# Dilated attention on one core: which engine copies the result rows out of PSUM

## What is computed

```
for window, dilation in ((128, 1), (512, 4), (2048, 16)):
    # positions regrouped by residue mod dilation; a query sees the 128 keys before it and itself
    o_i, lse_i = dilated_window_attn(q, k, v, window, dilation)     # 12 heads of 64
    # inside: s = q k / 8, masked; m = max(s); p = exp(s - m); den = sum(p); lse = m + log(den); o = (p / den) v
mix_w = softmax(stack(lses), axis=0)
o = sum(mix_w[..., None] * stack(outs), axis=0)
attn_out = o * silu(g_attn)
```

## Time and profile before

| | |
|---|---|
| median of 3 runs | 2197.28 us (2194.53 to 2199.95) |
| the profiled execution, time | 2200.2 us |
| the profiled execution, span | 2198.3 us |
| mean granted clock of TensorE | 0.97 of full speed |
| PE busy | 2008.3 us (91%) |
| DVE busy | 1551.7 us (71%) |
| ACT busy | 982.3 us (45%) |
| POOL busy | 997.2 us (45%) |

### The profile page before, as it was taken

One profiled execution on the slowest core, in us unless ns is written; L12 is line 12 of the kernel. 1 busy time (PEld: TensorE's weight loads), 2 busy tenths in 40 slices (PEclk: granted clock), 3 DMA queues, 4 the chain that ended last, 5 costly groups with the idle time before them and its releaser, 6 DMA issues.

```text
span 2198.3 us, 44066 instructions
## 1 busy us (share of the span) xinstructions
PE 2008.3 (91%) x16552; PEld 1487.1 (68%) x16552; DVE 1551.7 (71%) x3563; ACT 982.3 (45%) x2123; POOL 997.2 (45%) x1064
## 2 busy tenths in 40 slices
PE   5999999997788999689999999999998988786998
PEld 3545867896787888579864443447877777665886
DVE  7714948856898456687968889564499999894422
ACT  4323334321787001233443444333299999782211
POOL 4312324364331899631444333343124888974222
PEclk9999999999899999899999999999999999998999
DMA  5451331246661334332232232114367878565442
GB/s 180 138 125 58 102 94 37 66 139 197 159 140 42 124 139 151 122 125 69 70 107 78 75 93 72 56 50 112 90 143 174 203 195 207 162 191 166 163 167 85
DMA packets 275859, 267.40 MB, mean 122 GB/s; under 512 B 38224, under 2 KB 227536, under 8 KB 275392
## 3 DMA queue, kind: packets, MB, share of 16 engines
q1 hardware_dynamic: 266992, 252.19, 40.3%
q10 hardware_dynamic: 6976, 6.90, 1.2%
q0 software_dynamic: 1680, 5.51, 0.7%
HBM read 171.22 MB, written 93.31 MB: 120 GB/s over the span
## 4 chain that ended last, share of the span: by engine, by line
PE 37%; DVE 19%; POOL 10%; issue 5%; DMA 2%; ACT 2%; SPq 0%; DVEq 0%; ACTq 0%; POOLq 0%
PE bank L445 18%; PE bank L3072 7%; PE bank L173 7%; DVE s2m L2921 5%; DVE p2l L2927 4%; POOL xr L1995 2%; POOL xr L1993 2%; POOL xr L2008 2%; PE bank L1637 1%; POOL xr L2010 1%; PE bank L1654 1%; PE bank L1628 1%; DMA cm<-scr_part 1%; DVE ptl L1710 1%; DVE w2s L379 1%
## 5 line engine op out<-in xcount | busy, mean ns | idle before, releaser
L173 PE MATMUL bank<-w1h,xh 128*128 128x256 f16 x768 | 211.7, 276 | 3.0 <-DVE s1st L1169 3.0
L173 PE MATMUL bank<-w1h,xl 128*128 128x256 f16 x768 | 211.7, 276 | 0.0
L173 PE MATMUL bank<-w1l,xh 128*128 128x256 f16 x768 | 211.6, 276 | 0.0
L2866 PE MATMUL bank<-ident,p2r 128*128 128x128 f32 x900 | 163.9, 294 | 50.2 <-DVE p2l L2927 43.3
L2866 PEld LDWEIGHTS bank<-ident,p2r 128*128 128x128 f32 x900 | 95.9, 143 | 107.5 <-DVE p2l L2927 105.0
L2927 DVE SCALAR_TENSOR_TENSOR p2l<-bank,p2h 128x512 f16<-128x512 f32 (+1 forms) x288 | 165.0, 573 | 2.4 <-ACT p2h L2893 2.3
L1179 DVE SCALAR_TENSOR_TENSOR bank<-ain,cw,bank 128x512 f32<-128x512 f32 x208 | 157.0, 755 | 8.0 <-ACT bank L1124 1.7
L2921 DVE CUSTOM_DVE_ANT_0 s2m<-bank,both,finv 128x256 f32<-128x256 f32 (+1 forms) x384 | 161.1, 460 | 0.0
L173 PE MATMUL bank<-w2h,xh 128*128 128x256 f16 x512 | 140.5, 274 | 14.8 <-DVE xl L851 13.7
L2900 ACT ACTIVATE p2r<-s2m,ob 128x128 f32<-128x128 f32 (+1 forms) x384 | 147.5, 436 | 13.6 <-DVE ob L2921 13.3
L2893 ACT ACTIVATE p2h<-bank 128x512 f16<-128x512 f32 (+1 forms) x288 | 144.3, 501 | 15.1 <-PE bank L2866 11.5
(11 more groups left out here) (450 smaller groups left out, 6383.6 us busy)
## 6 DMA issues: line engine op xcount, KB each, us to landing
scr_part<-ob SPq DMA_DIRECT2D x48, 264.0 KB, 3.3
cm<-scr_part SPq DMA_DIRECT2D x48, 264.0 KB, 4.5
v<-scr_v SPq DMA_DIRECT2D x192, 65.0 KB, 2.4
ax<-in_x SPq DMA_DIRECT2D x16, 512.0 KB, 6.0
xr<-in_x SPq DMA_DIRECT2D x16, 512.0 KB, 4.4
bx<-scr_x SPq DMA_DIRECT2D x16, 512.0 KB, 8.0
x2r<-scr_x SPq DMA_DIRECT2D x16, 512.0 KB, 4.3
out<-yo SPq DMA_DIRECT2D x16, 512.0 KB, 2.9
```

The source lines that it names most:

```text
L173: ins = nc.tensor.matmul(dst, x, y, start=k == 0 and m == 0, stop=k == n - 1 and m == 2)
L2866: ins = nc.tensor.transpose(bank[:, w * hh + 128 * c:w * hh + 128 * c + 128], p[:, hh, 128 * c:128 * c + 128], ident[:])
```

## The change

ACT now makes the row copies of all units with dilation 1 and 4. With dilation 16 the two engines go on taking turns.

```
             elif item[0] == "gather":
                 x = units[item[1]]
                 if x["g"] % 2 == 0:
-                    on_act = x["g"] % 4 == 2
+                    on_act = x["d"] < 16 or x["g"] % 4 == 2
                     n_row[not on_act] += 1
                     o_bank = obk.take(a_row.at(n_row[0]) if on_act else d_row.at(n_row[1]))
```

## The result

The changed kernel takes 2190.85 us, the median of 14 runs (2187.01 to 2197.22), against 2198.51 us for the kernel before, also of 14 (2194.53 to 2203.91). The ratio is 0.9963, with a 95% interval of 0.9953 to 0.9974: 7.7 us less, where 11.0 were forecast. It is faster by a little more than the 0.3% that a measurement of this kernel can tell. The profiled execution has a span of 2189.8 us, against 2198.3.

A forecast was written before the change was run, and what follows sets the result against it. VectorE was taken to bound the stage of dilated attention. By pair of heads the gains were 2.3 + 2.0 + 5.4 + 1.3 = 11.0 us, subtracted from the median of 2197.28: 2186.3 us, range 2181.0 to 2193.5.

The forecast's parts named there:

- ScalarE sets the pace: Rival: ScalarE bounds every group at its upper ends, no reserve used; 6.0 us won, 2191.3 us; chance 0.21.
- The price on VectorE: Each row copy on VectorE puts off its successor by 0.33 us; 48 copies give an upper bound of 16.0 us.
- The price on ScalarE: On ScalarE a copy costs 0.26 us; four units take 5.64 to 5.74 (dilation 1), 5.22 to 5.32 (dilation 4).
- 0.77 us to spare: Reserve between ScalarE's p2h ending and VectorE's p2l taking it up, which ScalarE's lag must first use up: 0.77 us.
- I take 0.4: First pair of heads, without mixes: ScalarE's lag less the reserve costs 0 to 0.5 us, taken as 0.4.
- Dilation 16 gives ScalarE time to catch up: In dilation 16 the split is unchanged, so ScalarE recovers its lag and only the first pair of heads pays.
- Second: 2.0: Second pair of heads: GpSimd still waits for VectorE; six copies count, the last two are lost, 2.0 us won.
- Third to fifth: 1.8 each: Third to fifth pairs of heads: three copies win 1.0 us, then GpSimd's waits allow 0.79: 1.8 each, 5.4 together.
- E and B of dilation 16: Mix steps on VectorE, reciprocal and min: VectorE waits 0.3 to 0.7 us more for GpSimd there from the second pair.
- the 0.79 that GpSimd was to leave between the two B: Between the mins of dilations 4 and 16, GpSimd's waits for VectorE, 0.24 + 0.55 us, limit the gain to 0.79.
- I take the middle, 1.3: Sixth pair of heads: 0 won if GpSimd sets the way until 1969 us, otherwise 2.67; the middle, 1.3, taken.
- nothing changes: Rival: a copy costs ScalarE its whole 370 ns; 2.6 us won at most, 2194.7 us; chance 0.06.

The follow-up runs named there:

- light runs: Two of the three weight products of each mix left out on GpSimd: in the kernel before 2190.39 us, in the changed kernel 2182.30 us.
- after_again: The changed kernel run once more, unaltered, as a base for later runs: 2191.28 us, 0.9972 of the kernel before.
- d1_only: Against the kernel before, only the copies of dilation 1 go to ScalarE (24 instead of 48), dilation 4 stays split: 2191.19 us, 0.9967.
- d4_only: Against the kernel before, only the copies of dilation 4 go to ScalarE: 2195.66 us, 0.9981.
- lead_11: The changed kernel with GpSimd's query copies issued 11 steps ahead instead of 12: 2194.02 us, 0.9979 of the kernel before.
- q_one: The changed kernel with 8 of 96 query copies, in the stretch at the end, moved from GpSimd to ScalarE, one instruction each: 2185.15 us, 0.9940.

## Why the prediction was right, and where its sizes were off

The direction and the mechanism held. VectorE was the bound of the stage, the copies were on its path, and ScalarE had nearly the room for them. The size was less well met: 7.7 us lie below the 8.5 to 13.5 that the prediction gave to its own forecast (chance 0.58), and within the 3 to 8.5 that it gave to the rival "ScalarE sets the pace" (0.21). The time, 2190.85 us, is in the range of 2181.0 to 2193.5 because that range takes in both. It is 4.6 us above the forecast of 2186.3, of which 1.2 come from the median before, now 2198.51 and not 2197.28.

- **The price on VectorE, 0.33 us a copy.** Right: a pattern of dilation 1 with three copies in its window went from 22.96 to 21.96 us. The 1.3 us named as a sign counted all four copies; the fourth lies in the window of dilation 4.
- **The price on ScalarE.** Right, at the lower end: pressed, exps are followed by p2h after 0.80 us, and four units of dilation 4 take 5.21 us (forecast 5.22). The rows are from the changed kernel's first pair:

```profile
1607.43 0.97 ACT L2900 ACTIVATE p2r<-s2m,kept 128x256 f32<-128x256 f32 x2
1608.23 0.66 ACT L2893 ACTIVATE p2h<-bank 128x512 f16<-128x512 f32 x1
...
1616.52 1.02 ACT L2900 ACTIVATE p2r<-s2m,ob 128x256 f32<-128x256 f32 x2
...
1621.73 1.05 ACT L2900 ACTIVATE p2r<-s2m,ob 128x256 f32<-128x256 f32 x2
...
1629.07 0.79 ACT L2893 ACTIVATE p2h<-bank 128x512 f16<-128x512 f32 x1
```

- **"0.77 us to spare" and "I take 0.4" for the first pair.** Mis-sized: 2.67 less the 1.55 won is 1.1 lost. All of it stands before six p2l, at 1607, 1619, 1624, 1629, 1631 and 1635 us, 0.06 to 0.40 us each. The 0.77 is the reserve at a step with full keys. A unit with half the keys shortens VectorE's step by 0.27 us while the p2h it will ask for is still a full one. And while ScalarE runs without a gap the durations of its instructions grow: p2h lasts 0.60 us in the earlier trace rows and 0.79 us at 1629.07, with the distances between starts unchanged, so its result comes later than the starts suggest. VectorE's wait right after it:

```profile
1629.88 0.69 DVE L2927 SCALAR_TENSOR_TENSOR p2l<-bank,p2h 128x512 f16<-128x512 f32 x1 [0.32 <-ACT p2h L2893]
```

- **"Dilation 16 gives ScalarE time to catch up."** Only after nine microseconds: in the first pair ScalarE runs without a gap until 1637, and that pattern grew by 0.42 us. In the pairs with mixes, where I had put ScalarE at nothing, 0.2 to 0.4 us are lost before p2l where dilation 4 passes to 16, in the light runs and in the changed kernel.
- **"Second: 2.0."** 1.66 won. In dilation 16 VectorE waits 0.47 us for GpSimd at E, which the two copies counted as lost (0.67 us) cover. Right behind it come 0.30 us for ScalarE's exps, for which the sum had nothing:

```profile
1692.54 0.20 DVE L2949 RECIPROCAL ce<-ce 128x8 f32<-128x8 f32 x1 [0.47 <-POOL ce L2791]
1693.05 0.35 DVE L2921 CUSTOM_DVE_ANT_0 s2m<-bank,mask,finv 128x128 f32<-128x128 f32 x1 [0.30 <-ACT p2r L2900]
```

- **"Third to fifth: 1.8 each."** Mis-sized, 1.3 to 1.5. E and B of dilation 16 behaved as forecast: together they take 0.65 us more than before in pair 3, within the 0.3 to 0.7 named. The term that failed is the 0.79 that GpSimd was to leave between the two B. I had used the exclusion of the Trainium skill (SBUF — State Buffer, section "SBUF: two separate sides") on the B of dilation 16 only, and not on the one before. VectorE came to that B before GpSimd's query copy was through. The rows are B of the third pair in dilation 4 and GpSimd's query copy, after:

```profile
1743.19 0.67 DVE L2944 TENSOR_TENSOR ce<-kept,cm 128x8 f32<-128x8 f32 x1
1743.90 0.17 DVE L2946 TENSOR_TENSOR ce<-ce,cm 128x8 f32<-128x8 f32 x1
```

```profile
1742.71 1.12 POOL L2963 COPY qs<-qn 128x512 f16<-128x512 f16 x1
```

and before:

```profile
1748.88 0.16 DVE L2944 TENSOR_TENSOR ce<-kept,cm 128x8 f32<-128x8 f32 x1
```

```profile
1747.65 1.12 POOL L2963 COPY qs<-qn 128x512 f16<-128x512 f16 x1
```

  Before, the min came 0.11 us after the copy's end (1748.77). After, it came 0.48 us into it and ended with it, at 1743.86: 0.5 us lost in each of the three pairs. Such a hold shows as a longer duration of VectorE's row and not as a wait. Further on VectorE waits 0.31 us at E, and the min in dilation 16 is held for 1.06 us, where one of the two was held for 0.90 before (1763.49). The first two rows are these; the other two are for the last pair:

```profile
1754.10 0.20 DVE L2949 RECIPROCAL ce<-ce 128x8 f32<-128x8 f32 x1 [0.31 <-POOL ce L2791]
...
1758.09 1.06 DVE L2944 TENSOR_TENSOR ce<-kept,cm 128x8 f32<-128x8 f32 x1
...
1894.56 0.20 DVE L2949 RECIPROCAL ce<-ce 128x8 f32<-128x8 f32 x1 [4.04 <-POOL ce L2791]
...
1936.37 0.20 DVE L2949 RECIPROCAL ce<-ce 128x8 f32<-128x8 f32 x1 [0.72 <-POOL ce L2791]
```

- **"I take the middle, 1.3" for the last pair.** 0.24 won in the one profile of the changed kernel, and 1.14 in the other. The last two rows show what holds it. VectorE still waits about 4 us for GpSimd before the pair, as in the earlier trace rows, and comes to a new wait at E in the middle of the pair; both stand in after_again too. Between the two profiles lies a wait for the load of a mix in dilation 4:

```profile
1937.31 0.17 DVE L2944 TENSOR_TENSOR ce<-kept,cm 128x8 f32<-128x8 f32 x1 [0.73 <-DMA cm<-scr_part]
```

  It is absent from after_again, and the kernel before has it with 0.43 us. d1_only and d4_only, with half of the change each, won 0.44 and 0.28. Where between 0.2 and 1.1 us the gain of the full change usually lies stays open. The middle was a guess: one question, who sets the way between two waits, decided the whole term, and I had not answered it.
- **The rivals.** "ScalarE sets the pace in every group" named a part of the mechanism, and its 6.0 us are nearer to the 7.7 than the 11.0 are. Its price was off: ScalarE was at its lower end. In the first pair it does cost 0.13, 0.14 and 0.40 us in the last three groups of dilation 4, which the prediction had named as a sign against itself; from the second pair on it costs almost only at the turn to dilation 16. That nothing changes, with a copy at its full duration of 370 ns, was refuted by the distance of 0.26 us, which held when ScalarE was full.

## What to carry to other kernels

When two engines pass work to and fro, moving an instruction from the full one to the other wins its start-to-start distance, until the other is as full. From there reserves decide, and they have to be taken at the shortest step, not at a typical one, and again when the engine runs without a gap. Before moving work in a loop that a third engine serves, ask what the faster engine will now arrive in the middle of. Here 1.5 us, against 7.7 won, went into a tiny min that came half a microsecond too early in three pairs. And half of the edit, dilation 1 alone, had most of its value.

## What the runs showed of the hardware that I had not expected

- A min of 8 columns on VectorE was held for the whole of a GpSimd copy (1.02 us in lead_11), when it came 0.1 us after the copy's start. An order that seemed to put the copy out of the way made the hold longer.
- Copying 512 float16 columns costs ScalarE 1.04 us from start to start where the source has a stride of 16 elements (dilation 16), and 0.56 with a stride of 4 (q_one). GpSimd's copies in the kernel before show 1.08 and 0.60. A row copy of 260 float32 columns costs ScalarE 0.26.
- ScalarE's instructions last up to 0.2 us longer when it runs without a gap, at unchanged distances between their starts, and VectorE gets the result at the end of the longer duration. Why they lengthen is not shown.
